# GpSimd's weight mixes tied to a fixed unit, hidden tile 7 summed last, and modulation steps taken in pairs, in a two-layer recurrent decoder trunk

## The chip, the cores and the metric

The kernel runs on one core of one Trainium2 chip. The metric is the device time of one execution in microseconds; lower is better. Of several executions the median is quoted.

## What is computed

A prompt of 512 tokens and 8 sample sequences of 8 tokens (T = 576 columns together) go through two layers. A layer is a half-step feed-forward block, a mixer (gated DeltaNet and RWKV-7 heads in layer 0, GLA and mLSTM heads in layer 1), and a second half-step feed-forward block. Each block begins with an RMS norm whose shift and scale, and ends with a gate, that come from a small conditioning product ("modulation"):

```python
cs = silu(c)                                       # (1 + 8 sequences, 1024)
for l in range(2):
    mod = (cs @ w_mod[l] + b_mod[l]).reshape(c.shape[0], 9, 1, 1024)
    h = rms(x) * norm_gain[l, 0] * (1 + mod[:, 1]) + mod[:, 0]
    f1 = (silu(h @ w_ffn_gate[l, 0]) * (h @ w_ffn_up[l, 0])) @ w_ffn_down[l, 0]
    x = x + 0.5 * (1 + mod[:, 2]) * f1
    h = rms(x) * norm_gain[l, 1] * (1 + mod[:, 4]) + mod[:, 3]
    x = x + (1 + mod[:, 5]) * mixer_l(h)           # even: delta + RWKV-7, odd: GLA + mLSTM
    h = rms(x) * norm_gain[l, 2] * (1 + mod[:, 7]) + mod[:, 6]
    f2 = (silu(h @ w_ffn_gate[l, 1]) * (h @ w_ffn_up[l, 1])) @ w_ffn_down[l, 1]
    x = x + 0.5 * (1 + mod[:, 8]) * f2
y = rms(x) * final_gain
```

The width is 1024 (KT = 8 tiles of 128 rows), the feed-forward width 2816 (FT = 22 tiles). The new recurrent states are returned too.

## The kernel before

Everything lies feature by feature on the 128 partitions, with tokens along the columns. The dense products are made by `dense_chain`, which takes a list of stages ("up", "down", "out", "proj_even", "proj_odd") and writes the instruction streams of all engines in one order. A stage is cut into units (one output tile of 128 features, for both halves of the token columns or for one), a unit into pieces (one weight block each: up has a gate and an up block, down has three, of 8, 8 and 6 hidden tiles, and a projection one). A product in full precision is made of three reduced ones: every weight block and every token tile is split into a high part by ScalarE (`split_high`, line 170) and a low part by VectorE (`split_low`, line 174), and TensorE sums low x high, high x low and high x high (lines 1500, 1502, 1504).

The pieces are numbered through the whole chain, and each engine walks over them: while TensorE works on piece i, ScalarE and VectorE split piece i + 2 (`AHEAD`) into one of three places; a place is free when the piece that used it is done (`piece_done`). SyncE loads raw weight blocks into three buffers (`RAW`), each as soon as the split that read it is through. Each engine runs its own queue strictly in the order in which the program writes it.

**Up stages.** There are four. Tiles are made in the order 8 to 21, then 0 to 7 (`UP_FIRST`). The first four tiles are plain. The 18 others are "sevens": the four blocks of a tile's gate and up weights are made with seven half-size products in place of eight, from sums of weight blocks and of token blocks. The weight sums are the four GpSimd additions of lines 1361 to 1369 ("the mixes"): the first three give a block of 1024 columns, the unit's second piece, and change the raw up block in place, and the fourth gives its fourth piece of 512 columns. TensorE makes the seven products on lines 1402 to 1404; a unit is 84 of them, in pieces of 24, 24, 24 and 12. VectorE adds the products (lines 1794, 1800, 1802, 1806), ScalarE takes the silu (1597), and `gate_up_sums` (line 1815) writes the hidden tile and raises `act_done`. The first sevens' token sums are split just before they are first used; the last of them (`t4`) is needed in the second half of the third piece.

**Hidden tiles.** The down projection needs each hidden tile split too. Tiles 1 to 7 (`IN_TIME`) are split right when they are made (`split_act`, `low_act`). Tile 0 and tiles 8 to 21 (`LATE`) are kept raw in `big_buf` and split at fixed pieces near the end of the stage: 0; then 8 and 9; 10 to 12 at the last piece; and 13 to 15, 16 to 18 and 19 to 21 at the first three pieces of the down projection, on both engines behind the weight split that stands at the same piece.

**Down stages.** Unit m = 0 waits tile by tile for `act_low_done` or `late_low`; TensorE sums the hidden tiles in the order 0 to 21.

**Modulation.** `Modulation` makes the next block's modulation row, in 16 steps (`MOD_STEPS`): a step is one 768 KB load into a buffer and four products of 384 columns on the four column groups of the array (line 122; eight records in the profile). Five stages carry it, three down and two input projections. Step s stands behind piece `stage.first + 1 + s`; its buffer (three in a down stage, two in a projection) is reused by a later load that waits for `done`.

## Time and profile before

| | |
|---|---|
| median of 3 runs | 2722.47 us (2714.78, 2722.47, 2723.15) |
| the profiled execution | 2715.64 us |
| its span, first to last instruction | 2713.9 us |
| TensorE matmul busy | 2586.4 us, 95% |
| VectorE busy | 1722.8 us, 63% |
| ScalarE busy | 1063.4 us, 39% |
| GpSimd busy | 641.3 us, 24% |
| mean granted TensorE clock | 0.968 of full speed |

The rows come from one profiled execution. PE is TensorE, PEld its weight loads, DVE VectorE, ACT ScalarE, POOL GpSimd, SP SyncE. L174 is line 174 of the kernel. Matmuls are pipelined: a record of a 288-column product lasts some 0.29 us while the next starts after 0.13, so idle time between two records is shorter than the time that is lost. "x2" means that two like instructions are merged into one row. A wait is shown in brackets with the idle time in us and what ended it.

### The profile page before, as it was taken

To read this page: it belongs to the slowest core of one execution; us is meant where nothing else is said; L and a number is where in the kernel's file an instruction comes from. 1 tells how busy PE (TensorE), PEld (TensorE's weight loads), DVE (VectorE), ACT (ScalarE), POOL (GpSimd) and SP (SyncE) were. 2 spreads that over 40 slices of the span, in tenths; PEclk is the share of its full clock that TensorE was granted. 3 is DMA by queue.
4 is the path that set the end of the run, shared out by engine and by line. 5 is a ranking of instruction groups with operands and counts; after the bars stand their busy time and mean duration, and the time that the engine had idled before them with its cause. 6 is when DMAs were issued, how large, how long until landed. Compare 5 with 4: busy or idle time off the path is not lost. (4 is left out here: it accounts for less than half of the span.)

```text
span 2713.9 us, 52764 instructions
## 1 busy us (share of the span) xinstructions
PE 2586.4 (95%) x22860; PEld 2413.2 (89%) x22860; DVE 1722.8 (63%) x2312; ACT 1063.4 (39%) x1542; POOL 641.3 (24%) x494
## 2 busy tenths in 40 slices
PE   6999999999988899999999999999999989999998
PEld 4999989887877787999989999988889879999997
DVE  5789725665465556799943689952644356789824
ACT  4444414454344323544432544432432334444513
POOL 0455101000010122155400065500100212355201
PEclk8999999999999979999999999999999789999999
DMA  6232455731100014222255322245662114222224
GB/s 233 101 125 93 147 184 157 268 121 55 34 3 3 18 74 159 86 86 96 90 202 164 107 91 94 94 171 179 201 220 71 42 51 141 69 96 93 90 82 131
DMA packets 81584, 306.84 MB, mean 113 GB/s; under 512 B 9145, under 2 KB 14793, under 8 KB 80073
## 3 DMA queue, kind: packets, MB, share of 16 engines
q1 hardware_dynamic: 81352, 303.47, 33.0%
q8 instruction: 181, 2.97, 0.4%
q14 instruction: 51, 0.41, 0.0%
HBM read 292.70 MB, written 10.74 MB: 112 GB/s over the span
## 5 line engine op out<-in xcount | busy, mean ns | idle before, releaser
L174 DVE TENSOR_TENSOR weights_r<-work,weights_r 128x1024 fp32r<-128x1024 f32 (+1 forms) x332 | 450.9, 1358 | 353.8 <-ACT weights_r L170 353.4
L170 ACT ACTIVATE weights_r<-work 128x1024 fp32r<-128x1024 f32 (+1 forms) x332 | 325.3, 981 | 574.4 <-PE banks L1504 350.1
L1385 POOL TENSOR_TENSOR rows<-rows,consts 128x288 f32<-128x288 f32 (+3 forms) x64 | 88.7, 1386 | 746.1 <-ACT consts L1635 741.6
L1500 PE MATMUL banks<-low_r,weights_r 128*128 128x288 f32 (+2 forms) x912 | 235.0, 305 | 18.6 <-DVE low_r L174 12.0
L1502 PE MATMUL banks<-low_r,weights_r 128*128 128x288 f32 (+1 forms) x1008 | 243.1, 299 | 0.0
L1502 PE MATMUL banks<-big_r,weights_r 128*128 128x288 f32 (+2 forms) x960 | 240.8, 298 | 0.0
L1402 PE MATMUL banks<-h_r,weights_r 128*128 128x288 f32 x768 | 227.5, 296 | 3.8 <-DVE weights_r L174 3.7
L1504 PE MATMUL banks<-low_r,weights_r 128*128 128x288 f32 (+2 forms) x912 | 229.4, 299 | 0.0
L1403 PE MATMUL banks<-big_r,weights_r 128*128 128x288 f32 x768 | 226.9, 295 | 0.0
L1404 PE MATMUL banks<-h_r,weights_r 128*128 128x288 f32 x768 | 226.6, 295 | 0.0
L174 DVE TENSOR_TENSOR ring_r<-consts,ring_r 128x1024 fp32r<-128x1024 f32 (+1 forms) x104 | 132.3, 1272 | 132.3 <-ACT ring_r L170 132.3
L1500 PE MATMUL banks<-h_r,weights_r 128*128 128x288 f32 (+1 forms) x832 | 205.7, 306 | 9.1 <-DVE big_r L440 8.5
L1504 PE MATMUL banks<-h_r,weights_r 128*128 128x288 f32 (+1 forms) x832 | 199.2, 299 | 0.0
L1500 PEld LDWEIGHTS banks<-low_r,weights_r 128*128 128x128 f32 x912 | 158.6, 192 | 41.5 <-issue 22.2
L170 ACT ACTIVATE ring_r<-consts 128x1024 fp32r<-128x1024 f32 (+1 forms) x104 | 105.1, 1010 | 176.2 <-PE banks L1504 146.6
L1502 PEld LDWEIGHTS banks<-low_r,weights_r 128*128 128x128 f32 x1008 | 172.4, 190 | 0.2
L1402 PE MATMUL banks<-low_r,weights_r 128*128 128x288 f32 x576 | 170.1, 295 | 0.0
L1403 PE MATMUL banks<-low_r,weights_r 128*128 128x288 f32 x576 | 169.9, 295 | 0.0
L1500 PEld LDWEIGHTS banks<-h_r,weights_r 128*128 128x128 f32 x832 | 140.6, 189 | 32.9 <-issue 11.3
L1404 PE MATMUL banks<-low_r,weights_r 128*128 128x288 f32 x576 | 169.4, 294 | 0.0
L1502 PEld LDWEIGHTS banks<-big_r,weights_r 128*128 128x128 f32 x960 | 167.2, 191 | 0.3
L1504 PEld LDWEIGHTS banks<-low_r,weights_r 128*128 128x128 f32 x912 | 159.3, 192 | 0.0
(577 smaller groups left out, 6948.5 us busy)
## 6 DMA issues: line engine op xcount, KB each, us to landing
work<-w_ff_dram SPq DMA_DIRECT2D x118, 512.0 KB, 3.4
h<-w_mod_dram SPq DMA_DIRECT2D x48, 768.0 KB, 5.2
work<-w_down_dram SPq DMA_DIRECT2D x66, 512.0 KB, 3.6
consts<-w_ff_dram SPq DMA_DIRECT2D x58, 512.0 KB, 3.4
big_buf<-w_mod_dram SPq DMA_DIRECT2D x24, 768.0 KB, 5.9
work<-w_mod_first_dram SPq DMA_DIRECT2D x24, 512.0 KB, 12.2
work<-w_in_even_dram SPq DMA_DIRECT2D x24, 512.0 KB, 3.3
consts<-w_down_dram SPq DMA_DIRECT2D x22, 512.0 KB, 3.7
```

Of the source, the lines that this page charges most:

```text
L170: return act.activation(high, raw, ACT.Copy)
L174: return engine.tensor_tensor(low, raw, high.bitcast(F32), ALU.subtract)
L1385: pool.tensor_tensor(k.rows[:, c], k.rows[:, c], k.square[:, c], ALU.add).then_inc(added, 1)
L1402: pe.matmul(out, low[:, w], x_high, start=j == 0, stop=False)
L1403: pe.matmul(out, high[:, w], x_low, start=False, stop=False)
L1404: last = pe.matmul(out, high[:, w], x_high, start=False, stop=j == KT // 2 - 1)
L1500: pe.matmul(out[a], low[:, w], x[a][0], start=begins, stop=False)
L1502: pe.matmul(out[a], high[:, w], x[a][1], start=False, stop=False)
L1504: last = pe.matmul(out[a], high[:, w], x[a][0], start=False, stop=closes)
```

## The change

Three edits. `MOD_PAIRED` and `mod_steps_after` decide which modulation steps TensorE makes behind a piece: in a down stage, and from step 10 on in a projection, none behind an even step's piece and two behind an odd one's. `DOWN_ORDER` is the order in which a down projection sums the hidden tiles: 0 to 6, 8 to 21, then 7; the host lays the weights out in that order, and the waits and the tokens follow it. GpSimd gets one more wait, for `act_done` to reach `u.nth - 1`, that is for the hidden product of the unit two before the one whose weights it mixes.

```diff
+MOD_PAIRED = 10
...
+DOWN_ORDER = [*range(UP_FIRST - 1), *range(UP_FIRST, FT), UP_FIRST - 1]
...
+        def mod_steps_after(stage, step):
+
+            if step is None:
+                return ()
+            if stage.kind == "down" or step >= MOD_PAIRED:
+                return (step - 1, step) if step % 2 else ()
+            return (step,)
...
             if u.kind == "down":
-                pair = k.big_r[:, kt * T + lo:kt * T + hi], k.low_r[:, kt * T + lo:kt * T + hi]
-                return pair if kt in IN_TIME else pair[::-1]
+                tile = DOWN_ORDER[kt]
+                pair = k.big_r[:, tile * T + lo:tile * T + hi], k.low_r[:, tile * T + lo:tile * T + hi]
+                return pair if tile in IN_TIME else pair[::-1]
...
                             pool.wait_ge(*u.gate.landed)
                             pool.wait_ge(*u.up.landed)
+                            pool.wait_ge(act_done, u.nth - 1)
...
                             if u.kind == "down" and u.m == 0:
-                                up = up_before[stage]
-                                if kt in IN_TIME:
-                                    pe.wait_ge(act_low_done, in_time.index(up.of[kt, 0]) + 1)
+                                up, tile = up_before[stage], DOWN_ORDER[kt]
+                                if tile in IN_TIME:
+                                    pe.wait_ge(act_low_done, in_time.index(up.of[tile, 0]) + 1)
                                 else:
-                                    pe.wait_ge(late_low, late_count(up, kt))
+                                    pe.wait_ge(late_low, late_count(up, tile))
...
                         step = mod_step_after(stage, i)
-                        if step is not None:
-                            if step == 0:
+                        for now in mod_steps_after(stage, step):
+                            if now == 0:
...
-                            mod_in[stage].products(pe, step)
+                            mod_in[stage].products(pe, now)
...
-        "w_down": cat([tile_weights(i["w_ffn_down"][l, s]) for l in range(DEPTH) for s in range(2)]),
+        "w_down": cat([tile_weights(i["w_ffn_down"][l, s].reshape(FT, P, D)[DOWN_ORDER].reshape(DFF, D)) for l in range(DEPTH) for s in range(2)]),
```

On TensorE, in the first down projection, these are the last tile of the first piece (weights in `ring_r`) and the first row of the second piece (`weights_r`), before:

```order
L1500 MATMUL banks<-big_r,ring_r 128x300 [waits act_low_done_63]
L1500 MATMUL banks<-big_r,ring_r 128x276
L1502 MATMUL banks<-low_r,ring_r 128x300
L1502 MATMUL banks<-low_r,ring_r 128x276
L1504 MATMUL banks<-big_r,ring_r 128x300
L1504 MATMUL banks<-big_r,ring_r 128x276
L1500 MATMUL banks<-low_r,weights_r 128x300 [waits late_low_93,w_low_done_58]
```

and the same place in the changed kernel:

```order
L1512 MATMUL banks<-low_r,ring_r 128x300 [waits late_low_93]
L1512 MATMUL banks<-low_r,ring_r 128x276
L1514 MATMUL banks<-big_r,ring_r 128x300
L1514 MATMUL banks<-big_r,ring_r 128x276
L1516 MATMUL banks<-low_r,ring_r 128x300
L1516 MATMUL banks<-low_r,ring_r 128x276
L1512 MATMUL banks<-low_r,weights_r 128x300 [waits late_low_93,w_low_done_58]
```

The eighth tile was tile 7, which waits for `act_low_done`; it is tile 8 now, which waits for `late_low`.

At the end of the second piece of the same stage TensorE had the first modulation step (line 122), and behind it the third piece:

```order
L1504 MATMUL banks<-low_r,weights_r 128x300
L1504 MATMUL banks<-low_r,weights_r 128x276
L122 MATMUL banks<-h,cs 32x384 [waits mod1_landed0_129,modfirst_biased_109,act_done_61]
L122 MATMUL banks<-h,cs 32x384 x3
L1500 MATMUL banks<-low_r,weights_r 128x300 [waits late_low_93,w_low_done_58]
```

In the changed kernel the third piece follows the second directly, and it ends with tile 7 and two steps (line 123), ahead of the fourth piece:

```order
L1512 MATMUL banks<-big_r,weights_r 128x300 [waits act_low_done_63]
L1512 MATMUL banks<-big_r,weights_r 128x276
L1514 MATMUL banks<-low_r,weights_r 128x300
L1514 MATMUL banks<-low_r,weights_r 128x276
L1516 MATMUL banks<-big_r,weights_r 128x300
L1516 MATMUL banks<-big_r,weights_r 128x276
L123 MATMUL banks<-h,cs 32x384 [waits mod1_landed0_129,modfirst_biased_109,act_done_61]
L123 MATMUL banks<-h,cs 32x384 x3
L123 MATMUL banks<-h,cs 32x384 [waits mod1_landed1_130]
L123 MATMUL banks<-h,cs 32x384 x3
L1512 MATMUL banks<-low_r,ring_r 128x300 [waits w_low_done_58,part_added_91]
```

The step moved from behind the second piece to behind the third, together with the one that stood there, and tile 7 is the last tile of the third piece. VectorE's, ScalarE's and SyncE's queues hold the same instructions in the same order as before; on GpSimd only the wait is new.

## Rows read from the trace of the kernel before

**Rows 1.** The page, part 1: busy us (share of the span) xinstructions, by engine.

```profile
PE 2586.4 (95%) x22860; PEld 2413.2 (89%) x22860; DVE 1722.8 (63%) x2312; ACT 1063.4 (39%) x1542; POOL 641.3 (24%) x494
```

**Rows 2.** Timeline, PE, units near the first up stage's end: start, us, instruction [wait].

```profile
268.65 0.40 PE L1402 MATMUL banks<-h_r,ring_r 128*128 128x288 f32 x1 [0.50 <-DVE ring_r L174]
...
292.35 0.40 PE L1402 MATMUL banks<-h_r,weights_r 128*128 128x288 f32 x1 [0.48 <-DVE weights_r L174]
```

**Rows 3.** Timeline, DVE, gate_up_sums of two units earlier in that stage.

```profile
203.75 1.86 DVE L1815 TENSOR_TENSOR big_buf<-work 128x576 f32<-128x576 f32 x1
...
214.94 1.85 DVE L1815 TENSOR_TENSOR big_buf<-work 128x576 f32<-128x576 f32 x1
```

**Rows 4.** Timeline, PE, the eighth tile of the first down projection.

```profile
311.56 0.41 PE L1500 MATMUL banks<-big_r,ring_r 128*128 128x300 f32 x1 [2.25 <-DVE low_r L174]
```

**Rows 5.** Timeline, PE, a lone modulation step; four steps of 256 columns.

```profile
1373.07 0.42 PE L1504 MATMUL banks<-low_r,weights_r 128*128 128x288 f32 x2
1373.42 0.85 PE L122 MATMUL banks<-h,cs 128*32 128x384 f32 x8
1374.21 0.54 PE L1500 MATMUL banks<-low_r,ring_r 128*128 128x288 f32 x2
...
118.58 1.93 PE L122 MATMUL banks<-work,cs 128*32 128x256 f32 x32
120.44 0.40 PE L1402 MATMUL banks<-h_r,weights_r 128*128 128x288 f32 x1
```

**Rows 6.** Timeline, DVE, in a unit near the first up stage's end.

```profile
269.66 1.22 DVE L174 TENSOR_TENSOR weights_r<-work,weights_r 128x1024 fp32r<-128x1024 f32 x1
...
272.60 1.84 DVE L1815 TENSOR_TENSOR rows<-work 128x576 f32<-128x576 f32 x1
...
278.50 1.94 DVE L174 TENSOR_TENSOR weights_r<-work,weights_r 128x1024 fp32r<-128x1024 f32 x1
```

**Rows 7.** Timeline, DVE, gate_up_sums where GpSimd has no more mixes to make.

```profile
296.31 0.75 DVE L1815 TENSOR_TENSOR rows<-work 128x576 f32<-128x576 f32 x1
```

**Rows 8.** Timeline, POOL, the first and third addition of the unit of rows 6.

```profile
272.37 1.46 POOL L1361 TENSOR_TENSOR work<-work,consts 128x512 f32<-128x512 f32 x1 [4.86 <-DMA consts<-w_ff_dram]
...
275.68 1.69 POOL L1365 TENSOR_TENSOR work<-consts,work 128x512 f32<-128x512 f32 x1
```

**Rows 9.** Timeline, ACT, the high part of that unit's mixed block.

```profile
278.56 1.06 ACT L170 ACTIVATE weights_r<-work 128x1024 fp32r<-128x1024 f32 x1 [1.93 <-PE banks L1404]
```

**Rows 10.** The page, part 6: DMA issues, xcount, KB each, us to landing.

```profile
work<-w_ff_dram SPq DMA_DIRECT2D x118, 512.0 KB, 3.4
h<-w_mod_dram SPq DMA_DIRECT2D x48, 768.0 KB, 5.2
```

**Rows 11.** Timelines, POOL and DVE, at the first mixed unit of the third up stage.

```profile
1572.90 1.44 POOL L1361 TENSOR_TENSOR work<-work,consts 128x512 f32<-128x512 f32 x1 [3.33 <-DMA consts<-w_ff_dram]
...
1575.82 0.75 DVE L1782 TENSOR_TENSOR big_buf<-work,banks 128x576 f32<-128x576 f32 x1 [0.27 <-ACT work L1621]
...
1580.57 1.81 DVE L174 TENSOR_TENSOR big_r<-big_buf,h_r 128x1152 fp32r<-128x1152 f32 x1
```

**Rows 12.** Timeline, PE, the first product of that unit.

```profile
1574.94 0.30 PE L1402 MATMUL banks<-h_r,ring_r 128*128 128x288 f32 x1
```

**Rows 13.** Windows: us, busy (xinstructions) by engine, granted clock, DMA share, GB/s.

```profile
311.60:316.60 5.00, 5.00 (x26) 5.00 (x27) 4.71 (x7) 3.62 (x6) 0.00 (x0) 0.66 0.60 203
1366.00:1371.00 5.00, 4.96 (x37) 4.96 (x38) 4.70 (x7) 3.70 (x6) 0.00 (x0) 1.00 0.61 203
...
1093.90:1098.90 5.00, 5.00 (x37) 5.00 (x38) 4.55 (x9) 2.42 (x6) 1.51 (x1) 1.00 0.30 110
```

**Rows 14.** Timelines, PE and DVE, third piece of the last down projection.

```profile
2570.05 0.43 PE L1500 MATMUL banks<-low_r,ring_r 128*128 128x288 f32 x2
...
2573.35 0.40 PE L1500 MATMUL banks<-low_r,ring_r 128*128 128x288 f32 x1 [0.76 <-DVE big_r L174]
...
2572.54 2.09 DVE L174 TENSOR_TENSOR big_r<-big_buf,low_r 128x576 fp32r<-128x576 f32 x3
```

**Rows 15.** Timeline, PE, a shorter wait, between two blocks.

```profile
1093.90 0.40 PE L1500 MATMUL banks<-low_r,weights_r 128*128 128x288 f32 x1 [1.64 <-DVE work L1854]
```

## The prediction

> **What bounds the kernel now.** The page comes first: TensorE is busy for 2586 of 2714 us [rows 1], so only what makes TensorE stand still, run at its lower clock or change what it does between two products can move the end. Work on the other engines counts only where TensorE waits for it. I then read TensorE's own waits in time, at the three places the change touches. They fall into three families.
>
> First, near the end of each up stage. TensorE waits for a VectorE weight split at 268.65, at 280.50 and at 292.35 [rows 2]: two units in 23.70 us, 11.85 each. Earlier in the stage a unit takes 11.19 (one gate_up_sums at 203.75, the next at 214.94 [rows 3]), so a unit with the wait is 0.66 us too long. The pattern stands once in each of the four up stages, three full units each.
>
> Second, at the first piece of each down projection: TensorE is idle for 2.25 us at tile 7, for VectorE's low part of it [rows 4]. There are four such waits (2.21 to 2.25).
>
> Third, the modulation steps: a step inserted between two pieces takes TensorE from 1373.42 to 1374.21 [rows 5], 16 times in each of five stages.
>
> **Part A, the mixes begin after the hidden product two units back.** What makes the late units long is VectorE. In the unit at 272 us gate_up_sums takes 1.84 us [rows 6], while without GpSimd beside it it takes 0.75 [rows 7]. GpSimd's first addition starts at 272.37 [rows 8], 0.23 before it. TensorE's weights at 280.50 are ready only when the split that starts at 278.50 and takes 1.94 is through [rows 2, 6]. VectorE goes from split to split with no slack in these units; it is the bound there. With the new wait the first addition cannot start before gate_up_sums ends, so that one takes 0.75: VectorE's round shrinks by 1.1, from 11.85 to about 10.8, under the 11.19 that TensorE needs. What of the four additions overlaps the later splits was overlapping splits before, and the first addition now falls into VectorE's wait for ScalarE after gate_up_sums. So the units return to 11.19: 3 x 0.66 = 2.0 us a stage, **8.0 us gained** in all. Ends: 0 (the waiting only moves, a rival below) and 10 (a fourth, small wait per stage goes too).
>
> Who waits for GpSimd now? Its third addition ends at 277.37 today [rows 8], 5.0 after the first began. It would start 0.98 later (272.60 + 0.75 against 272.37) and end at about 278.4; ScalarE asks for it at 278.56 [rows 9]. The margin is small but there. Behind the new wait on GpSimd's queue stand only the additions of the same unit. The load that reuses the gate's buffer waits for the fourth one, about 1 us later than today; it lands in 3.4 us [rows 10] and is wanted about 4 us after its issue, when the next unit's additions start: no delay that ScalarE would see.
>
> The cost lies at the second mixed unit of each stage. Its mixes start at 1572.90 today; the hidden product they must now wait for (the last plain unit) is written at 1575.82 and takes 0.75 [rows 11], so they start at 1576.6 and run through VectorE's next splits. The first mixed unit's token split, 1.81 us at 1580.57 [rows 11], is needed in the middle of its third piece: the unit starts at 1574.94 [rows 12], and 60 of its 84 products (11.19 / 84 = 0.133 each) are before it, so at 1582.9; it is ready at 1582.4. Three additions now alternate with VectorE's three splits (1.2, 0.7, 1.3 us without GpSimd beside them), each side waiting for the other's running instruction: 1576.6 + 3 x 1.3 + 1.2 + 0.7 + 1.3 = 1583.7. TensorE is held for about 0.75 us, **3.0 us lost** over four stages. Ends: 0 (the order of the two falls luckily) and 2.1 each (one more addition of 1.3 in front). A comes to 5.0 gained.
>
> **Part B, tile 7 last.** The wait at 311.56 is 2.25 us idle; as a product's record (0.29) overlaps the next start (0.13 apart) the true loss is 2.4: 4 x 2.4 = 9.6 us. In two of the four the granted clock then falls: mean 0.66 over the five us from 311.6 (the same at 1786), against 1.00 at 1366 (the same at 2563) [rows 13]. That is the lower of the two levels for 3.4 us, half of which is lost: 2 x 1.7 = 3.4. Tile 7 now has two more pieces (12.5 us) to be split in, so both go.
>
> What is late next? Tile 19. Its split stands on ScalarE and VectorE behind the split of a later weight piece, which has to wait until TensorE has finished the second piece. In the last down projection the third piece starts at 2570.05, the low part of tile 19 is the first of the three VectorE records from 2572.54 (done at 2573.3), and TensorE, which asks for it as the fourth tile, restarts at 2573.35 [rows 14]: 0.94 late. In the other three stages the modulation step after the second piece hides this (in the first all but 0.2). The change takes both covers away: tiles move up by one place, so 19 is the third tile, asked for 2 x 0.785 = 1.57 after the piece starts, and no step follows the second piece. Ready at 3.3, so 1.7 us late, four times: 6.8. Gone with it is today's 0.94 + 0.2 = 1.1. Tile 16 moves into the second piece, where it is the eighth; VectorE has it about 0.6 us before, so I cost it at nothing. Net: 9.6 + 3.4 + 1.1 - 6.8 = **7.3 us gained**. Ends for the new wait: 0.94 (today's, a place later) and 2.5 (VectorE one split further behind). The host's re-ordered weights cost no transfer.
>
> **Part C, two steps together.** A lone step: the product before it starts at 1373.20, the next at 1374.21, 1.01 instead of 0.13 apart, and the product after that is late by 0.11 (0.54 against 0.42 for two) [rows 5]: 0.99 us. What a second step right behind the first costs is not in this trace for 384 columns; the nearest rows are four steps of 256 columns in one run, 118.58 to 120.44 [rows 5]. If a lone one of these takes 0.79 x 256/384 = 0.53, the other three take 0.44 each, which is 0.66 for 384 columns. A pair saves 0.99 - 0.66 = 0.33. Pairs: 8 in each of three down projections, 3 in each of two input projections, 30 in all: **9.9 us gained**. Ends of the second step's price: 0.44 (no dearer than with 256 columns) and 0.85 (the whole record of a lone step), so 16.5 and 4.2.
>
> A pair frees its buffers later, so the next loads start later, by up to a piece. On SP's queue a weight load stands behind each. A 768 KB load lands in 5.2 us [rows 10]; the products that use it are two pieces, 12.5 us or more, behind the point that frees it, and the weights behind it have three. No wait.
>
> **The sum.** 5.0 + 7.3 + 9.9 = 22.2 us. The profiled execution took 2715.6 (span 2713.9), so 2693.4. The three timed runs are 2714.8, 2722.5 and 2723.2: the profile sits with the lowest. The four average 2719.0, and I take 22.2 off that average and forecast **2697**.
>
> **Rivals.** (1) *The sharing only moves.* VectorE's two-input instructions meet GpSimd's additions wherever these stand, the late units keep their waits, and A is only the 3.0 lost: 14.2 gained, 2705. For it: a split already takes 1.94 where 269.66's takes 1.22 [rows 6]. Against it: the first addition would run while VectorE waits anyway. The Trainium skill (GPSIMD Engine Reference, section Key points) says that GpSimd shares its SBUF interfaces with VectorE, with contention for two-input instructions; it gives no place where that is cheaper, and by that rule alone the answer would be this rival's. The rows agree with the sharing, 1.84 against 0.75. Chance 0.15.
>
> (2) *Tile 19 drops the clock.* If the new waits are followed by the lower clock as those of 2.25 were, each costs 1.7 more: up to 6.8, 2704. Idle for 1.64 us at 1093.90, TensorE kept a clock of 1.00 after it [rows 13, 15], and the new wait is about 1.6 idle. Chance 0.10.
>
> (3) *Pairs save nothing*: the change of product shape is hidden already. 12.3 gained, 2707. The Trainium skill (TensorE: Matmul & The Clock Gate, section on what happens when you issue a matmul) says weight loads are pulled ahead of matmuls in flight, and by this the break behind a step would be free. The row has 0.79 and 0.11 there instead. Chance 0.05.
>
> (4) *Slower: the mixes come too late.* In the late units TensorE needs the mixed split at about 271.9 in a unit that starts at 268.65, and has it at 270.88 [rows 2, 6]: 1.0 of slack. If each addition queues behind a split (2.35 us, two instructions' length, instead of 1.3 to 1.7), the third ends at 273.35 + 3 x 2.35 = 280.4, 1.8 past ScalarE's 278.56 and 0.8 past the slack, in 68 units: 54 us, and A's 8.0 are lost: 2759. It decides once the third addition ends 1.2 us or more after ScalarE asks (1.0 of slack, and 14.2 / 68 = 0.2). For it: margins of tenths. Against it: only two of three additions meet a split. Chance 0.04.
>
> **How the numbers follow.** Mine has 0.66. The range 2684 to 2708 takes in its bounds (the second unit's wait absent and the cheap second step below; the dear second step and the higher base above) and rivals 1 to 3. A measurement of this kernel tells from no change about 0.3%, 8 us: faster means below 2714. Rivals 1 to 3 are faster too, though rival (1) with a dear second step is not surely: faster 0.92, within 0.04, slower 0.04.
>
> **What would show it.** Right: gate_up_sums at 0.75 us in every mixed unit; no TensorE wait for a split in the late units; a wait of some 0.75 for the token split in each stage's first mixed unit; no wait at tile 7 and one of 1.5 to 1.7 idle at tile 19, four times, with the clock at 1.00 behind it; steps in groups of 16 records, about 1.67 us from the product before to the product after. Wrong: late-unit periods still near 11.85, the clock down after tile 19, waits for a modulation load, or ScalarE waiting for GpSimd.

## The result and the profile after

| | before | after |
|---|---|---|
| runs, us | 2714.78, 2722.40, 2722.47, 2723.15 | 2680.66, 2689.85, 2690.06, 2696.00 |
| median | 2722.43 | 2689.95 |
| profiled execution | 2715.64 (span 2713.9) | 2689.85 (span 2688.1) |

The ratio is 0.9884, with a 95% interval of 0.985 to 0.9918: 22 to 41 us less. On a second chip, with more runs (below, `after_again`), it is 0.9905 (0.9883 to 0.9926), 20 to 32 us less. The forecast was 2697 in a range of 2684 to 2708.

The page's part 1 and its row of TensorE's clock, after:

```profile
PE 2564.6 (95%) x22860; PEld 2408.4 (90%) x22860; DVE 1616.7 (60%) x2312; ACT 1067.3 (40%) x1542; POOL 652.3 (24%) x494
...
PEclk8999999999989969999999999999999889999999
```

Against [rows 1], VectorE has the same 2312 instructions and 106 us less busy time; its waiting inside instructions, for GpSimd, is what went (66 of the 106 in gate_up_sums, whose 72 records are now all 0.75 or 0.76). TensorE has 22 us less.

**The late units.** TensorE's timeline, the first record of one unit and of the next, where [rows 2] had a wait of 0.5 before each:

```profile
268.06 0.29 PE L1414 MATMUL banks<-h_r,ring_r 128*128 128x288 f32 x1
...
279.24 0.29 PE L1414 MATMUL banks<-h_r,weights_r 128*128 128x288 f32 x1
```

11.18 us apart, and no record in between has a wait. VectorE's timeline in that unit, the counterpart of [rows 6]:

```profile
269.65 1.22 DVE L175 TENSOR_TENSOR weights_r<-work,weights_r 128x1024 fp32r<-128x1024 f32 x1
270.78 0.75 DVE L1827 TENSOR_TENSOR rows<-work 128x576 f32<-128x576 f32 x1
272.29 1.38 DVE L175 TENSOR_TENSOR low_r<-rows,big_r 128x576 fp32r<-128x576 f32 x1 [0.76 <-ACT big_r L171]
273.59 1.78 DVE L175 TENSOR_TENSOR ring_r<-work,ring_r 128x512 fp32r<-128x512 f32 x1
...
275.96 1.65 DVE L175 TENSOR_TENSOR weights_r<-work,weights_r 128x1024 fp32r<-128x1024 f32 x1
...
279.00 1.22 DVE L175 TENSOR_TENSOR weights_r<-work,weights_r 128x1024 fp32r<-128x1024 f32 x1 [0.23 <-ACT weights_r L171]
```

gate_up_sums takes 0.75 in place of 1.84. The counterpart of the split at 278.50 is the one at 275.96: it takes 1.65 where it took 1.94, and is through at 277.61, 1.6 before TensorE starts the next unit with its weights at 279.24. The split at 279.00 has idle time ahead of it: VectorE is no longer the bound. The 1.84 of before is a wait inside the record: GpSimd's addition had started at 272.37 and takes 1.30 when nothing is in its way, so it would end at 273.67, and 0.75 more is 274.42, just where gate_up_sums ended (272.60 + 1.84). GpSimd's and ScalarE's timelines, the counterparts of [rows 8] and [rows 9]:

```profile
271.75 1.30 POOL L1373 TENSOR_TENSOR work<-work,consts 128x512 f32<-128x512 f32 x1 [4.13 <-DVE rows L1827]
...
274.90 1.63 POOL L1377 TENSOR_TENSOR work<-consts,work 128x512 f32<-128x512 f32 x1
276.61 2.16 POOL L1381 TENSOR_TENSOR work<-work 128x512 f32<-128x512 f32 x1
...
277.90 1.06 ACT L171 ACTIVATE weights_r<-work 128x1024 fp32r<-128x1024 f32 x1 [2.12 <-PE banks L1416]
```

The first addition is released by gate_up_sums and not by a load any more. The third ends at 276.53, 1.4 before ScalarE asks for its result. From TensorE's first of the seven-product records to its last, the four up stages take 204.95, 200.67, 200.68 and 200.67 us, before 207.29, 203.10, 203.13 and 203.06: 9.6 less in all. The three full waits a stage are 12 x 0.69 = 8.3 of this; the rest is a smaller one in the unit ahead of them, which the prediction had in its bound.

**Tile 7 and tile 19.** At tile 7's old place TensorE has no wait. TensorE's timeline has this at tile 19, in the four down projections:

```profile
317.86 0.54 PE L1512 MATMUL banks<-low_r,weights_r 128*128 128x300 f32 x2 [1.83 <-DVE big_r L175]
...
1368.58 0.53 PE L1512 MATMUL banks<-low_r,ring_r 128*128 128x288 f32 x2 [1.56 <-DVE big_r L175]
...
1783.84 0.40 PE L1512 MATMUL banks<-low_r,weights_r 128*128 128x288 f32 x1 [1.54 <-DVE big_r L175]
...
2547.49 0.40 PE L1512 MATMUL banks<-low_r,ring_r 128*128 128x288 f32 x1 [1.56 <-DVE big_r L175]
```

Windows of 5 us behind the first of these and behind another wait of this stage (the clock is the column after POOL's, as in [rows 13]):

```profile
317.86:322.86 5.00, 5.00 (x28) 4.72 (x32) 1.36 (x3) 0.01 (x1) 0.00 (x0) 0.66 0.36 107
454.20:459.20 5.00, 4.25 (x31) 4.02 (x32) 3.73 (x7) 2.60 (x5) 0.00 (x0) 1.00 0.40 128
```

Behind the other three waits at tile 19 the clock stays at its upper level, 2.4 GHz.

**Pairs of steps.** TensorE's timeline around a pair, the counterpart of [rows 5]:

```profile
1371.60 0.43 PE L1516 MATMUL banks<-big_r,ring_r 128*128 128x288 f32 x2
1371.95 1.50 PE L123 MATMUL banks<-h,cs 128*32 128x384 f32 x16
1373.38 0.53 PE L1512 MATMUL banks<-low_r,weights_r 128*128 128x288 f32 x2
```

From the last product before (the second of its row starts at 1371.73) to the first one after it takes 1.65, where two lone steps take 1.01 each. Two lone steps also take the place of two spacings of 0.13 and make two products late by 0.11, a pair one of each. So a lone step costs 0.98 (1.006 - 0.133 + 0.106, the mean of 47 in the kernel before) and a pair 1.62 (1.650 - 0.133 + 0.106, the mean of 19): a pair saves 2 x 0.98 - 1.62 = 0.34. There are 30, 10.2 us. The expectations below price a pair at 0.36 (2 x 1.007 - 1.652), which leaves the spacing and the late product out.

**A measure that leaves much of the clock's chance out.** In two stretches of this program, the mixers of the two layers, TensorE's clock stays low for a different part of the time in every execution. The change touches neither. Windows over the same products of both kernels, from the first to the last product of each stretch, before:

```profile
743.47:1107.65 364.18, 327.42 (x5930) 284.27 (x5930) 221.03 (x412) 131.88 (x259) 69.25 (x67) 0.91 0.16 56
2121.98:2243.13 121.15, 108.96 (x1070) 92.16 (x1069) 62.55 (x182) 44.66 (x87) 24.54 (x56) 0.76 0.19 56
```

and after:

```profile
738.30:1104.61 366.31, 330.88 (x5929) 287.20 (x5929) 221.65 (x412) 131.80 (x258) 68.71 (x65) 0.90 0.16 55
2105.72:2221.96 116.24, 101.53 (x1070) 86.51 (x1069) 62.04 (x182) 44.74 (x87) 24.53 (x56) 0.82 0.20 58
```

Over all thirteen executions profiled here the first stretch takes 356.5 to 366.5 us and the second 116.2 to 125.8, whichever edit is in the kernel. I therefore give, beside each ratio, the **rest**: the span less these two stretches. Before: 2713.9 - 485.3 = 2228.6. After: 2688.1 - 482.6 = 2205.5. The change takes 23.1 us off the rest. The rest still has falls of the clock in it: its mean granted clock lies between 0.989 and 0.992 in the thirteen executions, which is up to 8 us of full-speed time between two of them, though not all of that is on TensorE's path. A difference of 1 to 3 us between two single rests is therefore not shown to be an edit's.

### The profile page after: what moved, and what is told of

Same layout as the page of the kernel before. It is cut to its first block and busy times, and to the rows that moved or that the text cites. A ratio compares the mean times of both kernels' runs of the same rounds, so it can differ in the third digit from the quotient of the medians.

```text
span 2688.1 us, 52767 instructions
## 1 busy us (share of the span) xinstructions
PE 2564.6 (95%) x22860; PEld 2408.4 (90%) x22860; DVE 1616.7 (60%) x2312; ACT 1067.3 (40%) x1542; POOL 652.3 (24%) x494
## 5 line engine op out<-in xcount | busy, mean ns | idle before, releaser
L175 DVE TENSOR_TENSOR weights_r<-work,weights_r 128x1024 fp32r<-128x1024 f32 (+1 forms) x332 | 424.6, 1279 | 396.3 <-ACT weights_r L171 396.0
L175 DVE TENSOR_TENSOR ring_r<-consts,ring_r 128x1024 fp32r<-128x1024 f32 (+1 forms) x104 | 125.8, 1209 | 137.6 <-ACT ring_r L171 137.5
## 6 DMA issues: line engine op xcount, KB each, us to landing
work<-w_mod_first_dram SPq DMA_DIRECT2D x24, 512.0 KB, 12.5
```

The lines of the kernel that those rows point to most:

```text
L175: return engine.tensor_tensor(low, raw, high.bitcast(F32), ALU.subtract)
```

## The experiments

All of them, with the median of each, its ratio to the kernel before, run beside it (medians 2717.06 for the first four, 2717.59 for the next four, 2715.75 for the last three), and the profiled execution's span and rest:

| kernel | median | ratio (95%) | span | rest |
|---|---|---|---|---|
| mix_alone | 2700.05 | 0.9944 (0.9926 to 0.9962) | 2699.4 | 2218.3 |
| tile7_alone | 2706.68 | 0.9975 (0.996 to 0.999) | 2697.9 | 2219.7 |
| pairs_alone | 2711.77 | 0.9975 (0.996 to 0.999) | 2706.8 | 2222.3 |
| late_early | 2682.77 | 0.988 (0.986 to 0.9899) | 2681.7 | 2198.7 |
| after_again | 2691.93 | 0.9905 (0.9883 to 0.9926) | 2691.3 | 2205.5 |
| late_early_again | 2685.08 | 0.9881 (0.9859 to 0.9903) | 2683.8 | 2198.3 |
| late_first_pair | 2682.03 | 0.9869 (0.9844 to 0.9893) | 2679.9 | 2196.4 |
| pairs_all | 2685.04 | 0.989 (0.9863 to 0.9916) | 2678.6 | 2205.3 |
| late_pairs | 2677.70 | 0.9872 (0.985 to 0.9894) | 2673.4 | 2197.0 |
| late_loads | 2683.01 | 0.9885 (0.9865 to 0.9904) | 2678.2 | 2195.8 |
| late_pairs_loads | 2682.50 | 0.9884 (0.9864 to 0.9904) | 2677.5 | 2194.0 |

### The three parts one by one

**mix_alone**, the kernel before with the new wait alone:

```diff
                             pool.wait_ge(*u.up.landed)
+                            pool.wait_ge(act_done, u.nth - 1)
```

> Only GpSimd's new wait. My theory: the late in-time units (three full ones in each of four up stages) go from 11.85 to about 11.16 us with no wait of TensorE for a weight split, 12 x 0.69 = 8.3 us gained; and no wait for the token split t4 in the first mixed unit, as the changed kernel shows none (two additions stand in front of that split, not the three of my prediction). So about 8 us, ratio 0.997, and the tile-7 waits stay at 2.2 each. Rival, as the prediction had it: t4 is late by 0.75 in each stage, 5 us gained. Rival 'the sharing only moves': the late units stay at 11.85 and nothing is gained, ratio 1.000.

Measured: 15 us (10 to 20) by the ratio, 10.3 by the rest. TensorE has no wait between 76 and 300 us, so neither the late units nor a first mixed unit is held, and the four up stages take 204.95, 200.67, 200.68 and 200.67 as in the changed kernel. The 8.3 are there, 9.6 with the smaller waits. So is something no theory had: the wait at tile 7, which this edit should leave alone, is shorter. TensorE's timeline there, and then the window behind it:

```profile
308.89 0.54 PE L1501 MATMUL banks<-big_r,ring_r 128*128 128x300 f32 x2 [1.51 <-DVE low_r L174]
```

```profile
308.89:313.89 5.00, 5.00 (x37) 5.00 (x38) 4.69 (x7) 3.66 (x6) 0.00 (x0) 1.00 0.78 252
```

1.51 in place of 2.25 [rows 4], 1.46 to 1.51 in the four, with no fall of the clock behind any. VectorE's low part of tile 7 starts at 308.07 here and at 310.75 before, 2.68 sooner, while TensorE itself is only 1.93 ahead: part of tile 7's lateness was VectorE's backlog from the units before it. So A's wait is also worth 4 x 0.74 = 3.0, and in this execution two falls of the clock, until B takes the whole wait away. Such a fall costs less than the 1.7 that the prediction took: from the product at tile 7 to the next wait for a weight split the kernel before needs 142.92 and 146.35 with a fall (first and third down projection), this one 141.48 and 144.93 without, 1.4 less each. The rival "the sharing only moves" is refuted: the ratio's interval ends at 0.9962. The Trainium skill (GPSIMD Engine Reference, section Key points) has the sharing of the SBUF interfaces, and the rows agree that it is there; that it costs less at one place than at another, 1.84 or 0.75 for the same instruction, is not in that section, but in the rows.

The gains named here are 9.6 + 3.0 + 2 x 1.4 = 15.4, and the rest, 10.3, falls 5.1 short. Against them stand 1.6 more of wait for the first modulation load of the first projection (2.21 against 0.57), a fall of the clock at 475.1 behind it, and waits that the kernel before did not show: 0.75 at 459.11, 0.85 at 468.87, 0.58 at 1510.86 and 1.22 at 1531.61. They stand behind two places where the clock fell in the kernel before and not here, 3.4 us that this execution gained there (see "What the sum left out" below). The terms are named, but do not close to a microsecond.

**tile7_alone**, the kernel before with the down projections' order and the host's re-ordered weights alone:

```diff
+DOWN_ORDER = [*range(UP_FIRST - 1), *range(UP_FIRST, FT), UP_FIRST - 1]
...
-                pair = k.big_r[:, kt * T + lo:kt * T + hi], k.low_r[:, kt * T + lo:kt * T + hi]
+                tile = DOWN_ORDER[kt]
+                pair = k.big_r[:, tile * T + lo:tile * T + hi], k.low_r[:, tile * T + lo:tile * T + hi]
...
```

> Only the order of the down projection's tiles. My theory: the four waits of 2.2 at tile 7 go (9.6 us) and with them two falls of the clock (3.4); tile 19, now asked for third, is covered by the lone modulation step after the second piece in three stages (about 0.7 late there instead of the 1.6 to 1.8 of the changed kernel) and is 1.6 idle in the last down projection, which has no steps. 9.6 + 3.4 + 1.1 - 3 x 0.7 - 1.7 = 10.3 us gained, ratio 0.996. Rival: the step does not cover it and all four are 1.6, 7.3 us gained.

Measured: 7 us (3 to 11) by the ratio, 8.9 by the rest, of which 1.4 is not the edit's: two of the three late waits of the first up stage are missing in this execution. In the last down projection, which has no steps, the stretch from the up stage's last product to the end is 2.1 shorter (157.13 against 159.25), 2.4 in the changed kernel; the prediction's terms give 2.4 + 0.94 - 1.7 = 1.6 there. TensorE's timeline at tile 19, second and last down projection:

```profile
1361.56 0.41 PE L1502 MATMUL banks<-low_r,ring_r 128*128 128x288 f32 x1 [0.57 <-DVE big_r L174]
...
2556.99 0.41 PE L1502 MATMUL banks<-low_r,ring_r 128*128 128x288 f32 x1 [1.56 <-DVE big_r L174]
```

0.82, 0.57 and 0.56 where a lone step stands behind the second piece, 1.56 where none does: the step covers a microsecond of the wait, and taking it away (part C) costs that microsecond three times. The rival of four times 1.6 falls.

**pairs_alone**, the kernel before with `mod_steps_after` alone:

```diff
-                        if step is not None:
+                        for now in mod_steps_after(stage, step):
```

> Only the paired modulation steps. My theory: 30 pairs at 1.652 instead of 2 x 1.007 us, 10.9 gained; tile 19 loses its cover in three stages and is 0.8 to 0.9 idle there as it is in the last one before (2.6 lost); the first modulation load of the projection after the down projection lands later than it is wanted and costs up to 1.5. Sum 7 to 8 us gained, ratio 0.997; the tile-7 waits stay. Rival 'a pair saves nothing': the records of a pair would span 2.0 from the product before to the product after, and the kernel would be 3 to 4 us slower.

Measured: 7 us (3 to 11) by the ratio, 6.3 by the rest. Tile 19 (there still the fourth tile of its piece) waits 0.98, 0.77 and 0.74 in the three stages that lost their cover, as expected. The load did not cost what I had expected of it: no wait in the first projection and 0.31 in the second, while mix_alone, which has no pair at all, waits 2.21 and 1.16 there. Pairs are not what makes TensorE wait for that load.

2.4 of the 6.3 is not the edit's either, and says more of part A than of part C. The second up stage takes 200.67 here in place of 203.10, with no late wait, though GpSimd has no new wait in this kernel. VectorE's and GpSimd's timelines in a late unit of it:

```profile
1302.71 0.75 DVE L1824 TENSOR_TENSOR rows<-work 128x576 f32<-128x576 f32 x1
...
1302.77 1.85 POOL L1370 TENSOR_TENSOR work<-work,consts 128x512 f32<-128x512 f32 x1 [5.15 <-DMA consts<-w_ff_dram]
```

In three late units running the addition, released by a load, began 0.06, 0.45 and 0.30 us behind the start of gate_up_sums. Of the 72 records of gate_up_sums in this trace, the 57 that start while an addition is running take 1.84 to 1.86, the 15 others 0.75 or 0.76. So what decides is which of the two begins first, and the new wait fixes it: in the ten executions of kernels with it all four up stages take the shorter time.

The three rests add up to 10.3 + 8.9 + 6.3 = 25.5 against 23.1 together. They needn't be equal: A and B both take tile 7's lateness, the late waits that are missing by chance in tile7_alone and pairs_alone are counted in A too (3.8), B and C share the cover of tile 19, and these are single executions in which one load's wait differs by 2 us.

### The wait at tile 19

**late_early**, the changed kernel with one edit to where hidden tiles are split:

```diff
-                                 (end + 2, (16, 17, 18)), (end + 3, (19, 20, 21))):
+                                 (end + 2, (16, 17, 18, 19, 20, 21))):
```

> The changed kernel with the splits of tiles 19, 20 and 21 put a piece earlier, behind those of 16 to 18, where ScalarE stands idle from 312.3 to 314.8 and VectorE from 313.9 to 315.9 in the changed kernel. My theory: what makes TensorE wait at tile 19 is only that its split stands behind a weight split that has to wait for the second piece; so all four waits go, 4 x 1.7 = 6.8, and in the first stage the fall of the clock behind it, 1.7: about 8 us under the changed kernel, that is 2681, ratio to before 0.985. Rival: six splits take 3.4 us on ScalarE and end at 313.9, VectorE's at 315.8, and push the next weight split back, so that TensorE waits for weights one piece later: the sum is then within 3 us of the changed kernel's.

Timelines of ScalarE and VectorE in it, second piece of the first down projection:

```profile
310.81 3.54 ACT L171 ACTIVATE low_r<-big_buf 128x576 fp32r<-128x576 f32 x6
314.85 1.06 ACT L171 ACTIVATE weights_r<-work 128x1024 fp32r<-128x1024 f32 x1 [0.51 <-PE banks L1516]
...
312.08 4.10 DVE L175 TENSOR_TENSOR big_r<-big_buf,low_r 128x576 fp32r<-128x576 f32 x6
316.09 1.23 DVE L175 TENSOR_TENSOR weights_r<-work,weights_r 128x1024 fp32r<-128x1024 f32 x1
```

All six tiles are through before ScalarE may begin the next weight split, which still waits for TensorE; VectorE's starts 0.17 later than in the changed kernel (316.09 against 315.92). TensorE has no wait from 300 to 440 us, and none at tile 19 in any stage. The rest is 6.8 under the changed kernel's, and the medians are 7.2 apart (2689.95 and 2682.77). The two ratios, 0.988 and 0.9884, do not tell them apart, so both kernels ran once more beside each other on one chip.

**after_again** and **late_early_again**, the changed kernel and late_early unchanged:

> The changed kernel unchanged, on the chip of the next three. From its first trace: tile 19 idle 1.83 in the first stage and 1.54 to 1.56 in the other three, gains of the three parts 12 x 0.69 + 4 x 2.4 + 30 x 0.362 less 4 x 1.7, and with the clock about 25 us, ratio 0.991. If instead the 31 us between the medians is what the change gives, 0.988. The two attention stretches (743 to 1037 and 2109 to 2217 of the first trace), which the change doesn't touch, should differ by some us from run to run with the number of falls of the clock in them.

> The late splits a piece earlier, once more, now beside the changed kernel on one chip. Its first trace has no wait at tile 19 in any stage and no new one behind, 6.4 us less span. My theory: 6.8 and up to 1.7 less than the changed kernel, ratio of the two 0.997. Rival, that the two are the same since the ratios to before of the two calls were (0.988 and 0.9884): the time comes back as waits elsewhere.

Medians 2691.93 and 2685.08: 6.9 us apart, and no run of the one lies in the other's range but for 2686.64 and 2688.34. The rests are 2205.5 and 2198.3, each within 0.4 of its first execution, while the spans of the changed kernel differ by 3.2. Tile 19's waits, 7 us in all, come from a split's place on two queues and not from a lack of time on either engine. On the clock, after_again has the same wait as the changed kernel's first stage, and this in the window behind it:

```profile
317.46:322.46 5.00, 5.00 (x41) 3.82 (x42) 2.77 (x7) 1.17 (x2) 0.00 (x0) 1.00 0.35 110
```

Idle 1.82 and a clock of 1.00 after it, against idle 1.83 and 0.66. Likewise the wait of 2.18 at 454.20 was not followed by a fall, and the same one of 2.18 in the kernel before was. So the two falls that the prediction counted at tile 7 go with the wait, but whether one follows a given wait changes between executions.

A fall need not cost anything by the end of a stage either. These are windows behind the same wait, 2.17 and 2.19 for a weight split at the end of the first down projection, in late_early and in late_early_again:

```profile
451.10:456.10 5.00, 5.00 (x27) 5.00 (x28) 3.73 (x7) 2.60 (x5) 0.00 (x0) 0.66 0.40 127
...
451.06:456.06 5.00, 4.25 (x31) 4.03 (x32) 3.72 (x7) 2.60 (x5) 0.00 (x0) 1.00 0.39 128
```

The one at the lower clock has 0.9 of further waits up to 570 us, the other, at full clock, 4.1 (0.75 for the next weight split, 0.83 for a GpSimd sum, 2.5 for modulation loads). The first reaches the mixer at 736.41, the second at 735.91, though the first had a second fall at 608. The first modulation load is issued 10.66 behind the wait and has landed at 17.48 in the first, 11.65 and 19.81 in the second, so the first step comes 17.61 behind the wait at the lower clock and 19.94 behind it at full clock. Why the load goes out and lands later where the clock stayed up was not followed up.

### Modulation steps in the input projections

**pairs_all**, the changed kernel with `MOD_PAIRED = 0`: all steps of both projections in pairs.

> The changed kernel with all sixteen steps of both input projections paired (ten more pairs' halves, 5 pairs a stage). By the price of a pair 10 x 0.36 = 3.6 us and the first load's wait of 2.2 are gained. Against it the two buffers there: a load pair is issued when a pair has been used and its second one lands 7 to 8.5 us later, while the next pair is asked for 2 pieces of 3.3 plus 1.65 = 8.2 us later, so each pair could wait up to 1. My theory: no gain, between 3 us faster and 5 us slower than the changed kernel, with waits for w_mod loads in the trace before the pairs. Rival (loads never matter): 5.8 us faster and no waits.

Measured: 2685.04, 6.9 under after_again, but in the rest 2205.3 against 2205.5: the profiled execution's mixer stretches, which the edit does not touch, are 12.5 shorter. From an up stage's last product to the mixer, where the edit stands, it takes 437.4 and 337.6 in the two layers, the changed kernel's two executions 436.9 and 437.7, and 338.0 twice, so no gain shows. SyncE's issues and TensorE's timeline at the second pair:

```profile
474.43 0.33 SPq L116 DMA_DIRECT2D big_buf<-w_mod_dram  x1
476.39 0.33 SPq L1297 DMA_DIRECT2D work<-w_in_even_dram  x1
476.76 0.43 SPq L116 DMA_DIRECT2D big_buf<-w_mod_dram  x1
...
481.75 0.85 PE L123 MATMUL banks<-big_buf,cs 128*32 128x384 f32 x8
483.62 0.85 PE L123 MATMUL banks<-big_buf,cs 128*32 128x384 f32 x8 [1.02 <-DMA big_buf<-w_mod_dram]
```

The pair is broken in two by its second load. 2.3 us of such waits stand in the first projection. The rival that loads never matter falls; leaving steps 0 to 9 of a projection unpaired cost the change nothing that can be seen.

**late_first_pair**: late_early, with `not 2 <= step < MOD_PAIRED` in place of `step >= MOD_PAIRED`, so that steps 0 and 1 are paired too.

> As late_early, and steps 0 and 1 of the two input projections' modulations are paired too (steps 2 to 9 stay single). The first load is waited for by 2.05 and 0.19 idle in the changed kernel's two projections, and by 0.2 and 1.0 in late_early's; with the pair both are asked for a piece later (3.3 us), so these waits go, and 2 x 0.36 with them. Sum 2 to 3 us less than late_early. Rival: the third load starts a piece later and step 2 then waits, and nothing is gained; it is issued at about 479 then and lands in 5.5 to 6.4, while step 2 is asked for at about 482.

Measured: 2682.03 against 2685.08, and 1.9 less rest, near what was expected, though within what two executions can differ by. But not for my reason: the waits do not go, they stand inside the first pair (1.24) and before step 2 (0.73), 2.0 in all where late_early_again had 2.5.

**late_pairs**: late_early with `MOD_PAIRED = 0`.

> late_early with all steps of both input projections paired. If the two effects add, as pairs_all against the changed kernel was 2.3 to 6.9 us faster (by the two profiled spans 12.7, of which 12.5 lie in the attention stretches that neither touches), this is 2 to 5 us less than late_early: about 2681, ratio 0.9865. The waits before and inside the pairs stay: 1.2, 1.0 and 0.7 in the first projection's second to fourth pair, 0.3 and 0.1 in the other's.

**late_loads**: late_early, each modulation load one place earlier on SyncE's queue:

```diff
-                        step = i - stage.first - 4
+                        step = i - stage.first - 3
```

> late_early with each modulation load one place earlier on SP's queue, pairs as in the changed kernel. The first load of the first projection is issued at 465.53 in the changed kernel, 0.4 behind a weight load that stands before it, and lands in 8.1 among three weight loads; one place earlier it could go out some 2 us sooner. My theory: the wait for it, 2.0 to 2.3 in three of the traces so far, goes or falls under 0.5, and the later ones stay away: 0 to 3 us less than late_early. Rival: the load only shares the DMA engines with the weights in another order, the landing moves by less than 1 us and a wait for weights takes its place: no difference.

**late_pairs_loads**: both.

> Both edits together. In pairs_all the second load of a pair is issued at 476.76, 2.0 after the step that frees its buffer, since a weight load stands before it on the queue (476.39). One place earlier it goes out when its buffer is free, so the waits inside the pairs (1.2, 1.0, 0.7, 0.3, 0.1: 3.3 in all) fall under 1, and all of 10 x 0.36 = 3.6 and of the first load's wait is kept: 3 us less than late_pairs, 5 to 8 less than late_early, about 2678, ratio 0.985. Rival: the second load's landing time (7 to 8.5 beside weights), not its issue, makes the waits; they stay and it equals late_pairs.

TensorE's waits in the first projection of late_loads, in the wait view, which had 2.1 for a load in the changed kernel:

```profile
PE banks L1512 <- DVE low_r L442: 1.2, 1, 1.2
```

Its first load is issued at 460.19 in place of 465.53, and TensorE has no wait for a load any more; but a wait of 1.2 for VectorE's low part of the tokens stands there, so both theories were half right (late_early's first execution, whose clock fell ahead of it, has this wait too, with 0.9, and none for a load). The rest is 2.7 under the mean of late_early's two, late_pairs's 1.5, where 2 to 5 were expected. late_pairs waits 2.0 for loads there and 1.3 in the other projection; with the loads earlier these are 1.2 and none, again with a wait for L442 in their place (0.8 and 0.2). The rests are 2197.0 and 2194.0, the 3 us expected and no more than two executions can differ by; the medians (2677.70 and 2682.50) stand the other way round, and their mixer stretches differ by 7 us. These three kernels and late_first_pair can't be told apart by their medians. All lie under the changed kernel, whose gain of 7 us by late_early is the part that is shown; the rest measure has late_pairs_loads lowest, 11.5 under the change.

## Why the prediction was right, and where it was not

**Base.** The forecast was the mean of four runs of the kernel before, 2719.0, less 22.2. The rest fell by 23.1. The measured 2690 lies 7 under the forecast; of that 1 is the rest, and the other 6 are put down to the spread of the medians and not shown singly: on the second chip the medians of the same two kernels are 25.7 apart, not 32.5.

**A, 5.0 forecast.** The up stages gave 9.6: 12 x 0.69 = 8.3 in the late units against 8.0, and 1.3 by the smaller waits, left out of the sum. The step that failed is the cost: "three additions now alternate with VectorE's three splits", 0.75 late for the token split in four stages, 3.0 lost. The rows of the changed kernel, GpSimd and VectorE in the first mixed unit of the third stage (it starts at 1567.00):

```profile
1568.86 2.36 POOL L1373 TENSOR_TENSOR work<-work,consts 128x512 f32<-128x512 f32 x1 [4.89 <-DVE big_buf L1794]
1571.29 1.65 POOL L1375 TENSOR_TENSOR consts<-consts 128x512 f32<-128x512 f32 x1
1573.03 2.29 POOL L1377 TENSOR_TENSOR work<-consts,work 128x512 f32<-128x512 f32 x1
...
1568.83 1.23 DVE L175 TENSOR_TENSOR weights_r<-work,weights_r 128x1024 fp32r<-128x1024 f32 x1 [0.19 <-ACT weights_r L171]
...
1572.63 1.53 DVE L175 TENSOR_TENSOR big_r<-big_buf,h_r 128x1152 fp32r<-128x1152 f32 x1
```

The mixes start 3.9 later against the unit than before (3.7 was worked out). But only two additions start before the token split, and the split is through at 1574.16, 7.16 into the unit, where it is needed at 7.98. The prediction let three in. The other end of its bound, nothing lost, was what happened. A smaller slip: the first addition does not start 0.98 later in the unit, since gate_up_sums itself comes at 2.72 into the unit and no longer at 3.95, once VectorE is not behind. The margin to ScalarE was 1.4, not 0.2, so rival (4) was further off than its price made it look.

**B, 7.3 forecast.** Tile 7's wait went in all four stages. Tile 19 was forecast 1.7 late with 1.5 to 1.7 idle: 1.54 to 1.56 in three, 1.83 in the first, whose products have 300 columns (why it is longer there was not followed up). Rival (2) came true once in four in one execution and not in the next.

**C, 9.9 forecast.** A pair saves 0.34 where 0.33 was forecast: 30 x 0.34 = 10.2. The estimate of the second step, 0.66 from 256 columns scaled up, was 0.64. As a check, from tile 19 to the next weight split that is waited for, tile7_alone with 15 lone steps needs 135.1 in the second and in the third down projection, the changed kernel with 8 pairs 133.5; the prices give 15 x 0.98 - 8 x 1.62 = 1.7, measured 1.6. Rival (3) is refuted by the rows of the pair: the break stands once before and once behind sixteen records, not between the two steps. By the Trainium skill (TensorE: Matmul & The Clock Gate, section on what happens when you issue a matmul) weight loads are pulled ahead of the products in flight, which would leave no break; the rows have 0.22 in place of 0.13 from the product before to the first record, and 0.24 in place of 0.13 behind the first product after them. No wait for a load was forecast, and one was named as a sign of being wrong. One of 0.57 became 2.06, but mix_alone shows that the pairs are not its cause: among the kernels whose first load and step stand where they did, it is 0 to 0.57 in the three executions whose clock fell behind the wait some 20 us ahead of it (before, pairs_alone, late_early), 2.06 to 2.31 in four of the five whose clock did not, and 0.89 in the fifth, tile7_alone. No experiment set the clock, so this is a reading of eight traces, and why it is so stays open.

**What the sum left out.** Behind the waits at 459.20 and 1510.94 the kernel before ran at the lower clock; the changed one did not. The window in the kernel before, and the first product in the changed kernel that then waits:

```profile
459.20:464.20 5.00, 5.00 (x27) 5.00 (x28) 3.73 (x7) 2.59 (x5) 0.00 (x0) 0.66 0.35 125
...
458.23 0.39 PE L1512 MATMUL banks<-low_r,weights_r 128*128 128x276 f32 x1 [0.75 <-DVE weights_r L175]
```

By itself this is worth 2 x 1.7 = 3.4. But waits came into view that the slow stretches had covered, or that did not arise behind them: 0.75 at 458.23 and 0.59 at 1506.06 for a weight split, 0.53 and 0.36 for a GpSimd sum, 1.51 at 1527.20 for a low part of the tokens, and the load's 1.5. In all thirteen executions the wait of 0.75 stands exactly where the clock stayed up (six), and is absent where it fell (seven).

Added up: 22.2 forecast, 4.6 more by A, 0.3 by C, 3.4 by these two stretches; 1.7 less by the fall at tile 19, 0.6 by falls at tile 7 that were worth 1.4 each, and 5.2 by the waits that came into view, while older ones of 0.52 and 0.37 went (0.9 more). That makes 23.9, and 23.1 was measured. The sum was right to 1 us because terms of 1 to 5 us of both signs lay in it, not because each was right. That is luck, and the largest of them is A's, whose loss of 3.0 did not come.

## What to carry to other kernels

When two engines hinder each other, look for the time at which one of them waits anyway and put the other's work there: one wait on GpSimd's queue took 104 us off VectorE's busy time (1722.8 to 1618.5 in mix_alone), and 9.6 us off TensorE's up stages. When a wait is removed, ask which step stood in front of the next late thing as its cover, and whether that thing is late for want of time or only for its place on a queue; here moving three splits one piece earlier, into idle time that both queues showed, gave back the 7 us that the change had left. Before a fall of the clock is priced, look at what TensorE meets next: where it would have waited anyway, a fall can cost nothing. Where parts of a program vary by more than the effect, subtract them by windows between the same instructions, compare what is left, and ask how much of the same chance is left in it.

## What was not expected of the hardware

TensorE's clock, after a wait of one and the same length at the same place (1.82 and 1.83; 2.18 and 2.18), fell in one execution and stayed in the other. The two mixer stretches, whose work no edit touches, took 356.5 to 366.5 and 116.2 to 125.8 in thirteen executions, the shortest with a higher mean clock than the longest (0.92 in 356.48 against 0.90 in 366.52, 0.82 in 116.24 against 0.73 in 125.81). Behind the wait of 2.2 at the end of the first down projection a fall cost nothing by the time the mixer began (a difference of 0.5 between the two executions of late_early), behind those of 2.25 at tile 7 it cost 1.4.

A 1024-column split on VectorE beside GpSimd's additions took 1.23, 1.65 or 1.94, and gate_up_sums 0.75 or 1.84, by where the additions began; an addition of 512 columns took 1.30 alone and 2.29 to 2.36 when it was issued just after a split had begun. In a late unit VectorE is busy 10.16 us now, against 11.06 before, with the same eleven instructions and the same four additions.
